# The expert step of a hybrid decoder layer, its order on five engines, and where the routing lists are written

## The reference

```python
def swiglu(x, wg, wu, wd):
    return (jax.nn.silu(x @ wg) * (x @ wu)) @ wd
...
    eidx, ew = route(h2d, w_router, router_bias)
    ffn = routed_experts(h2d, eidx, ew, w_exp_gate, w_exp_up, w_exp_down) + swiglu(h2d, w_sh_gate, w_sh_up, w_sh_down)
    return layer_norm(DEEPNORM_ALPHA * h + ffn.reshape(B, L, D), ln2_g, ln2_b)
```

## Time and profile before

| | us |
|---|---|
| median of 3 runs (lowest, highest) | 1830.36 (1829.62, 1830.92) |
| the profiled execution, its time | 1829.32 |
| its span in the trace | 1827.7 |
| trunk's last product ends, experts' first starts | 1015.7, 1016.9 |
| last gate-up product ends | 1714.1 |

### The profile page before, as it was taken

How to read it: one execution, slowest core, us unless ns; L and a number is a source line. 1 busy time by engine, 2 the same in 40 slices (tenths; PEclk the granted TensorE clock), 3 DMA queues, 4 the chain that set the end, 5 groups by cost and what they waited for, 6 DMA issues and landing times. The chain is left out here.

```text
span 1827.7 us, 26841 instructions
## 1 busy us (share of the span) xinstructions
PE 1750.7 (96%) x9506; PEld 1346.2 (74%) x9506; DVE 1078.4 (59%) x1711; ACT 692.7 (38%) x1110; POOL 322.8 (18%) x286
## 2 busy tenths in 40 slices
PE   7999999999999999999999968999999999999897
PEld 7999999999855556998876546676767767676532
DVE  3112442544346555655678537777777777777478
ACT  3112222222245455111111326565656656565222
POOL 0000320412100000001055512111121221121101
PEclk9999999999999999999999989999999999999998
DMA  6332543434213123634251789999999999999395
GB/s 212 96 94 79 167 121 113 147 104 134 89 50 93 46 59 143 233 108 149 70 214 28 271 282 352 392 383 402 403 392 389 387 397 388 396 388 372 142 421 236
DMA packets 131599, 408.55 MB, mean 224 GB/s; under 512 B 21748, under 2 KB 83348, under 8 KB 112916
## 3 DMA queue, kind: packets, MB, share of 16 engines
q1 hardware_dynamic: 107172, 337.93, 50.7%
q0 software_dynamic: 21472, 52.59, 7.5%
q10 hardware_dynamic: 2880, 17.04, 2.3%
HBM read 359.70 MB, written 67.80 MB: 234 GB/s over the span
## 5 line engine op out<-in xcount | busy, mean ns | idle before, releaser
L2501 PE MATMUL e_Y<-mixT,e_aT 128*128 128x512 f32 x544 | 252.0, 607 | 22.2 <-ACT e_aT L2343 22.2
L2510 PE MATMUL e_G<-w_lo,xT_hi 128*128 128x512 f32 x528 | 206.5, 391 | 0.0
L2501 PEld LDWEIGHTS e_Y<-mixT,e_aT 128*128 128x128 f32 x544 | 100.7, 195 | 125.2 <-issue 124.9
L2424 DVE TENSOR_TENSOR w_lo<-wb,e_w_hi 128x1024 fp32r<-128x1024 f32 x132 | 152.9, 1220 | 31.0 <-ACT e_w_hi L2352 31.0
L2424 DVE TENSOR_TENSOR w_lo<-wb,half_hi 128x1024 fp32r<-128x1024 f32 x128 | 148.3, 1220 | 32.5 <-ACT half_hi L2352 32.5
L1292 PE MATMUL banks<-x_hi,gw_hi 128*128 128x352 f32 x464 | 151.6, 327 | 1.4 <-DVE r_srg L1084 1.4
L181 PE MATMUL banks<-w_hi,x_hi 128*128 128x244 f32 x512 | 143.0, 279 | 9.9 <-DVE x_lo L235 8.8
L1292 PE MATMUL banks<-x_hi,gw_lo 128*128 128x352 f32 x464 | 148.8, 321 | 0.0
L1292 PE MATMUL banks<-x_lo,gw_hi 128*128 128x352 f32 x464 | 148.8, 321 | 0.0
L181 PE MATMUL banks<-w_hi,x_lo 128*128 128x244 f32 x512 | 142.1, 278 | 0.0
L181 PE MATMUL banks<-w_lo,x_hi 128*128 128x244 f32 x512 | 141.8, 277 | 0.0
(11 more groups left out here) (426 smaller groups left out, 3633.3 us busy)
## 6 DMA issues: line engine op xcount, KB each, us to landing
wb<-in_w_exp_gu SPq DMA_DIRECT2D x64, 2048.0 KB, 16.2
mixT<-in_w_exp_dn SPq DMA_DIRECT2D x68, 1024.0 KB, 10.8
yk<-d_y_rows SPq DMA_DIRECT2D x8, 3072.0 KB, 22.4
gw_sb<-in_w_gate SPq DMA_DIRECT2D x20, 512.0 KB, 6.6
d_proj<-o_sb SPq DMA_DIRECT2D x8, 1098.0 KB, 6.0
d_gateT<-r_g_out ACTq DMA_DIRECT2D x16, 528.0 KB, 2.6
pages<-in_cache_both SPq DMA_DIRECT2D x64, 128.0 KB, 2.0
wb<-in_w_exp_gu ACTq DMA_DIRECT2D x4, 2048.0 KB, 15.9
```

Of the source, the lines that this page charges most:

```text
L2424: v.tensor_tensor(w_lo[s][:, :, at_k, :], w_gu[s][:, :, at_k, :], w_hi[c][:, :, at_k, :].bitcast(F32), ALU.subtract).then_inc(w_lo_ok, 1)
L2501: mm = t_.matmul(Y[q][:], aT[:, c, k, :], w_d[:, s, k, q * 512:(q + 1) * 512], start=k == 0, stop=k == 1)
L2510: mm = t_.matmul(G[c], x[:, c, k, :], w[:, :, k, :], start=k == 0 and i == 0, stop=k == KD - 1 and i == 2)
```

## The change

Five things are altered.

1. PE's order: a pass is now G(e) with A(e-1) inside it, before the seventh of the eight K slices (`TURN_AT = 6`); then Y(e-1); then T(e+2). ACT and DVE follow: ACT rounds xT of e+1, copies Y(e-2), makes two casts of the weights of e+1, copies `aT`, makes the other two casts, then the sigmoid of e. DVE makes the rest of xT, copies its half of Y(e-2), makes `w_lo` and then the gate's products.
2. Scatters: 42 instead of 36 stand in trunk ahead of the gathers, and the last 12 after them, still in trunk. None is left in `experts`.
3. Trunk gathers four experts instead of three. In `experts` each gather is one further ahead.
4. Trunk's SP also loads the first four down weights and the two vectors of the last layer norm, which stood at the start of `experts`.
5. The overflow lists: SP loads all 52 that there could be, one after each refill of experts 8 to 59, each with a reading of `meta`. DVE waits for them before the pass of experts 60 to 63, not before that of 16 to 19. POOL waits for no list.

```diff
+            sp.dma_start(g1, a["ln2_g"].partition_broadcast(P)).then_inc(ln2_in, 16)
+            sp.dma_start(b1, a["ln2_b"].partition_broadcast(P)).then_inc(ln2_in, 16)
...
+            sp.wait_ge(up_done, 3)
+            sp.wait_ge(r_done, NT)
+            for s in range(4):
+                sp.dma_start(w_d[:, s].rearrange("p k n -> p (k n)"), a["w_exp_dn"][s]).then_inc(d_in[s], 16)
...
+            def listing(t):
+                for k in range(TOPK):
+                    g.indirect_dma_start(tok_list, bass.IndirectOffsetOnAxis(ap=slot_c[:, t, k:k + 1], axis=0), entry[:, t, k, :], None).then_inc(listed, 16)
...
+            for t in range(NT - 2):
                 if t % G == 0:
                     pool.wait_ge(slot_ok, t // G + 1)
-                for k in range(TOPK):
-                    g.indirect_dma_start(tok_list, bass.IndirectOffsetOnAxis(ap=slot_c[:, t, k:k + 1], axis=0), entry[:, t, k, :], None).then_inc(listed, 16)
+                listing(t)
             for s in range(3):
                 pool.wait_ge(h_out_s[s], 48)
             pool.wait_ge(l_done, NT // G)
-            for s in range(3):
+            for s in range(4):
                 pool.wait_ge(g_ok, s + 1)
                 g.indirect_dma_start(xg[s][:], None, h_rows, bass.IndirectOffsetOnAxis(ap=g_idx[s][:, 0:1], axis=0), bounds_check=XT - 1, oob_is_err=False).then_inc(x_in_e[s], 16)
+            listing(NT - 2)
+            listing(NT - 1)
...
-                for s in range(3):
+                for s in range(4):
                     v.tensor_copy(g_idx[s][:], list_g[:, s:s + 1]).then_inc(g_ok, 1)
...
-            for s in range(W):
-                down(s, s)
-            sp.dma_start(early[:, 0:D], a["ln2_g"].partition_broadcast(P)).then_inc(ln2_in, 16)
-            sp.dma_start(early[:, D:2 * D], a["ln2_b"].partition_broadcast(P)).then_inc(ln2_in, 16)
             more = quads(sp)
...
-                free = sp.snap(r * W + (s - W + 1))
+                free = at(sp, r, W, s - W + 1)
                 wait_alone(sp, gu_done, free)
                 gate_up(e, s)
                 wait_alone(sp, d_done, free)
                 down(e, s)
-            with sp.Fori(1, NE // W) as r:
+            def overflow_list(b):
+                first = number(sp, b, 1, LIST - P)
+                sp.dma_start(over[:, bass.ds(b, 1), :].rearrange("p o two -> p (o two)"), tok_list[bass.ds(first, P), :]).then_inc(over_in, 16)
+            for s in range(W):
+                refill(1, s, W + s)
+            sp.wait_ge(listed, 16 * TOPK * NT)
+            sp.wait_ge(over_clear, 1)
+            with sp.Fori(2, OVER // W + 2) as r:
                 for s in range(W):
                     refill(r, s, sp.snap(r * W + s))
+                    overflow_list(sp.snap(r * W + (s - 2 * W)))
+            for s in range(W):
+                refill(NE // W - 1, s, NE - W + s)
             with sp.Fori(NE // W, more + NE // W) as r:
                 for s in range(W):
                     refill(r, s, number(sp, sp.snap(r * W + (s - NE)), 0, NE - 1))
...
             for s in range(W):
-                gather(s + 4, (s + 3) % W, 2 * s if s else None)
+                gather(s + 5, s, 2 * s + 2)
                 if s >= 2:
                     put_rows(s - 1, s % 2, s - 2)
-                if s < 3:
-                    t = NT - 3 + s
-                    for k in range(TOPK):
-                        g.indirect_dma_start(tok_list, bass.IndirectOffsetOnAxis(ap=slot_c[:, t, k:k + 1], axis=0), entry[:, t, k, :], None).then_inc(listed, 16)
-            pool.wait_ge(listed, 16 * TOPK * NT)
-            pool.wait_ge(over_clear, 1)
-            with pool.Fori(0, more) as r:
-                for s in range(W):
-                    first = number(pool, pool.snap(r * W + s), 1, LIST - P)
-                    pool.dma_start(over[:, bass.ds(pool.snap(r * W + s), 1), :].rearrange("p o two -> p (o two)"),
-                                   tok_list[bass.ds(first, P), :]).then_inc(over_in, 16)
-                wait_alone(pool, over_in, pool.snap(r * (16 * W) + 16 * W))
...
-                    gather(at(pool, r, W, s + 4), (s + 3) % W, at(pool, r, 2 * W, 2 * s))
+                    gather(at(pool, r, W, s + 5), s, at(pool, r, 2 * W, 2 * s + 2))
                     put_rows(at(pool, r, W, s - 1), s % 2, (s - 2) % W)
...
-            gather(at(pool, r, W, 4), 3, at(pool, r, 2 * W, 0))
...
-            def rounded(s, n_in, c):
+            def rounded(s, n_in, c, part):
                 act.wait_ge(gu_in[s], n_in)
-                for j in range(4):
+                for j in (2 * part, 2 * part + 1):
                     s_.copy(w_hi[c][:, :, 2 * j:2 * j + 2, :], w_gu[s][:, :, 2 * j:2 * j + 2, :]).then_inc(w_hi_ok, 1)
...
             def four(r, last=False):
                 for s in range(W):
-                    c = s % 2
-                    turned_act(at(act, r, W, s - 1), c)
...
-                    turned(at(act, r, 2 * W, 2 * s + 2), c)
+                    c, n_in = s % 2, at(act, r, 16, 16 if s < W - 1 else 32)
+                    if not (last and s == W - 1):
+                        turned(at(act, r, 2 * W, 2 * s + 4), 1 - c)
                     kept(at(act, r, W, s - 1), c, at(act, r, 8 * W, 16 * (s // 2) - 16))
                     if not (last and s == W - 1):
-                        rounded((s + 1) % W, at(act, r, 16, 16 if s < W - 1 else 32), 1 - c)
+                        rounded((s + 1) % W, n_in, 1 - c, 0)
+                    turned_act(at(act, r, W, s), 1 - c)
+                    if not (last and s == W - 1):
+                        rounded((s + 1) % W, n_in, 1 - c, 1)
+                    gate(at(act, r, W, s + 1), c)
...
-                    if s == 0:
-                        take(at(dve, r, W, 3), 3, at(dve, r, 16, 0))
-                    else:
-                        take(at(dve, r, W, s + 3), s - 1, at(dve, r, 16, 16))
-                    gated(at(dve, r, W, s), 1 - c)
-                    turned(at(dve, r, W, s + 1), c)
+                    if not last:
+                        take(at(dve, r, W, s + 4), s, at(dve, r, 16, 16))
+                    if not (last and s == W - 1):
+                        turned(at(dve, r, W, s + 2), 1 - c)
...
                         residue(at(dve, r, W, s), (s + 1) % W, 1 - c)
-            with dve.Fori(1, 4) as r:
+                    gated(at(dve, r, W, s + 1), c)
...
-            dve.wait_ge(over_ok, 1)
+            dve.wait_ge(over_in, 16 * OVER)
...
-            with dve.Fori(4, more + (NE // W - 1)) as r:
+            with dve.Fori(NE // W - 1, more + (NE // W - 1)) as r:
...
-            def gate_up(n, c, s, n_in):
...
                 for k in range(KD):
+                    if k == TURN_AT:
+                        turn_act(at(pe, n, 1, -1), 1 - c, at(pe, n, 1, -2))
                     for i, (x, w) in enumerate(((xT_hi, w_hi[c]), (xT_hi, w_lo[s]), (xT_lo, w_hi[c]))):
                         mm = t_.matmul(G[c], x[:, c, k, :], w[:, :, k, :], start=k == 0 and i == 0, stop=k == KD - 1 and i == 2)
                 mm.then_inc(gu_done, 1)
...
+            pe.wait_ge(xT_act, 2)
+            turn(2, 16, None)
             pe.wait_ge(gu_in[1], 16)
-            pe.wait_ge(xT_act, 2)
             for k in range(KD):
+                if k == TURN_AT:
+                    turn_act(1, 0, 0)
                 mm = t_.matmul(G[1], xT[:, 1, k, :], w_gu[1][:, :, k, :], start=k == 0, stop=k == KD - 1)
             mm.then_inc(gu_done, 1)
-            turn_act(1, 0, 0)
+            down(1, 0, 0, 16, 0)
+            turn(3, 16, 1)
...
-                    c, now, last = s % 2, at(pe, r, 16, 16), at(pe, r, 16, 0)
-                    turn(s, c, now, at(pe, r, W, s - 2))
-                    down(at(pe, r, W, s - 1), c, (s - 2) % W, last if s < 2 else now, at(pe, r, W, s - 2))
-                    gate_up(at(pe, r, W, s + 1), c, s, now)
-                    turn_act(at(pe, r, W, s), 1 - c, at(pe, r, W, s - 1))
+                    c = s % 2
+                    gate_up(at(pe, r, W, s + 1), c, s)
+                    down(at(pe, r, W, s), 1 - c, (s - 1) % W, at(pe, r, 16, 16 if s else 0), at(pe, r, W, s - 1))
+                    if not (last and s >= 2):
+                        turn((s + 2) % W, at(pe, r, 16, 16 if s < 2 else 32), at(pe, r, W, s))
+            with pe.Fori(1, more + (NE // W - 1)) as r:
+                four(r)
+            four(pe.snap(more + (NE // W - 1)), last=True)
```

78 lines of the change are left out of this document (34 added, 44 removed).

## The result

The changed kernel takes **1817.65 us** (median of 5 runs, 1814.44 to 1822.42) where the kernel before takes 1830.36 (1826.36 to 1832.97): a ratio of **0.9936, 95% interval 0.9908 to 0.9963**. That is 12.7 us less, where I had forecast 20.8 less. The time is inside the range of 1802 to 1821, in its upper half.

What follows compares the result with a forecast made beforehand. PE bounds mid-stage, with DMA close to its end; the first steps lose 28.9 us through waits on POOL's lists. The terms -28.9 + 4.1 + 2.5 + 0.5 + 1.0 = -20.8 give 1809.5 us, range 1802 to 1821.

Steps and rivals of the forecast that it cites:

- Part 1: Experts' first six steps: with the lists out of POOL's way there, the 28.9 us lost go; -28.9 us.
- next in line: Experts' first steps: down weights, expert 4's gate-up weights and PE's first result rows, the next that could be late.
- Part 2: Trunk's end: POOL's twelve scatters behind the gathers make PE start experts later; +4.1 us, bounds 2.5 and 6.6.
- The clock: Start of experts: after PE's idle time its clock runs at the lower level; +2.5 us, bounds 0 and 3.1.
- Part 3: Order of a step in experts: two more transpose/product borders, 0.01 us in each of 66 steps; +0.5, up to 2.0.
- Part 4: Weight stream in experts: list loads on SP make it late by up to 5 us near the end; +1.0, bounds 0 and 5.
- the case: Whole kernel: the forecast's own sum, 1809.5 us, from 1804 to 1818 with all bounds together; chance 0.64.
- B: Rival, start of experts: the late start doesn't happen and the clock holds; 1803 to 1806 us, chance 0.10.
- A: Rival, later half of experts: the weight stream falls 11 us short, casts wait for `wb`; 1816 to 1826 us, chance 0.12.
- D: Rival, SP's queue: list loads hold up the weights and the kernel gets slower, about 1857 or 1841 us; chance 0.04.
- C: Rival, experts' first steps: a new wait for rows queued behind scatters and down weights; 1815 to 1823 us, chance 0.08.
- E: Rival, experts' first steps: the three waits for rows stay, coming from DMA contention; 1834 us or so, chance 0.02.

Runs made afterwards that it cites:

- first comparison: The changed kernel against the kernel before, ahead of the twelve follow-up kernels, on a chip without a recorded number; 1817.65 against 1830.36 us, ratio 0.9936.
- e4: The changed kernel's order of the step, with lists, scatters and down weights where the kernel before had them; ratio to the kernel before 0.9994.
- e6: The kernel before's order of the step and of the row gathers, with everything else as in the changed kernel; ratio to the kernel before 0.9990.
- e8: The changed kernel with 6 of the last 12 scatters in the experts' first three steps, two behind each gather; 1823.37 us, ratio to the kernel before 0.9926.
- e1: The changed kernel with its last 12 scatters in the experts' first three steps, four behind each gather; 1827.99 us, ratio to the kernel before 0.9937.
- e5: The changed kernel once more, with nothing but a comment added; 1837.14 us, ratio to the kernel before 0.9990.
- e9: The kernel before once more, with a comment added, in the last group; ratio to the same kernel 0.9983.
- e12: The changed kernel once more, in the last group; ratio to the kernel before 0.9969.
- e7: The changed kernel with the last 12 scatters four behind each of the experts' first three gathers and only the 4 needed lists loaded; ratio to the kernel before 0.9945.
- e11: The changed kernel with the last 12 scatters three behind each of the experts' first four gathers, only 4 lists loaded; 1824.73 us, ratio to the kernel before 0.9906.
- e2: The changed kernel with the four down weight loads (4 MB) back at the start of the experts; 1831.64 us, ratio to the kernel before 0.9959.
- the three groups: Twelve follow-up kernels in groups of four on chips 7, 14 and 4, each beside the kernel before, which took 1839.4, 1839.4 and 1839.9 us.

## Why the prediction was right, and where it was wrong

**Part 1, the first steps: right, -28.9.** In the first comparison all of it went. The lists did it and not the order (e4 and e6, each with one of the two). Of what I had named as next in line nothing came late: rows, down weights and gate-up weights were there in time.

**Part 2, the late start: the step that failed.** I had +4.1 with bounds of 2.5 and 6.6, and it is +11.1 (1027.97 - 1016.90). POOL's issuing was foreseen to end at 1018.2 plus 0 to 4, and it ended at 1019.4 (the last scatter starts at 1018.46 and takes 0.96). What I left out is that the trunk's exit is not open when POOL has issued its last indirect DMA, but 6.0 to 10.7 us after the start of that issue; in the sum "POOL ends at 1018.2" stood for the end of the drain. e8 and e1 show it by dose: with 12, 6 and 0 scatters behind the gathers PE idles for 9.4 (e5), 1.2 and 1.6 us at the exit. The record of before alone would have given it: my own sum has the last scatter start at 1018.2 + 1.6 - 1.3 = 1018.5, and 1018.5 + 7.2 + 1.2 - 1016.9 = 10.0.

The clock: 2.5 forecast. T took 1.94 instead of 1.04, and the 12 records of G(1) until A 6.92 instead of 5.15 (e1 has 5.15 without the idle time): 2.6, as forecast. What I had not booked is the other end: behind the stage the lower level lasted 3.4 us instead of 6.8, and the end of the program is 1.8 shorter.

**Part 3, the order: right.** Forecast +0.5. It is 66 x 0.02 = +1.3 in the steps and -0.9 in the last two, +0.4.

**Part 4, the weights: inside its bounds, but not at the place I had.** Forecast +1.0 with bounds 0 and 5, and 2.7 was measured, 0 to 4.7 in the other kernels with the same list loads. I had SP's gap as 5.2 us each time, and the loss near the stage's end, from a growing backlog. The gap is 5.4 at the median but goes up to 10.7, and 1.6 of the 2.7 us are lost in the three steps from 1139 to 1171, behind the largest gaps. The rest lies in ten steps between 1391 and 1523, ahead of which no gap is over 7 us; what made those longer is open. Nothing is lost after them. By the Trainium skill, "DMA: Bandwidth & Descriptors", Latency and other measured facts, the floor of a register load is 0.6 us; the smallest of the 52 gaps, each with two of them, is 3.9 us, so none of the readings here came near that floor. The landing times rise as in the earlier trace rows: gate-up loads landed after 10.5 us near 1095 and 21.8 at the median near 1610, where no step is longer than usual.

So -28.9 + 11.1 + 2.6 + 0.4 + 2.7 - 1.8 = -13.9, where the span has -14.0. That the time still fell into the case's own 1804 to 1818, at its upper edge, is in part luck: the late start passed its bound by 4.5 us, the other terms stayed inside theirs, and the 1.8 that came back was in no sum.

**The rivals.** B is excluded by the start. A and D ask for a loss of 11 us or more in the weight stream; no run has over 4.7. C and E would show waits for rows in the first steps, and there is none. None of them happened: the time came out between the forecast and A through a term that no rival held, the drain.

**What stays open.** In the two later groups that repeat it (chips 14 and 4) the same change is worth 0.1 and 0.3%, with intervals from -0.03 to 0.5%, so the 0.6% of the first comparison should not be carried to other chips. Where the gain went can be read: of the span's 14.0 us only 3.6 are left (e9 to e12), 7.8 less between Y(0) and Y(67), mostly because the kernel before loses less in its first steps, 1.4 more at the start of Y(0) and 1.2 less behind the stage. Why ACT stands there is not settled. It happens in all runs of the groups with three or more scatters in a step (e1, e4, e7, e9, e11; 3.7 to 10.5 us idle) and in none with two or none; and in all seven with scatters behind the gathers PE waits 2.2 to 4.1 us ahead of G(0) where the other five have 1.15. So scatters have a part in it, and the stop moves with them. They are not enough: the kernel before has six a step in the first comparison too, and no such wait stands in either of its traces. Which resource they share with ACT no run shows.

## What to carry to other kernels

Work moved ahead of a barrier is paid until the queue's drain has ended, 6 us or more behind the last issue here, and not until it has been issued. Before moving a queue's work to the end of a block, read when the drain of that queue ended in the trace of before, and whose end hides it. An idle moment made so can cost twice: behind the 12.7 us here the clock was at its lower level, which cost another 2.6 us. Work that nobody needs soon is best spread thin, a few DMAs a step, rather than put on either side of a border: with six there and two a step PE idled 1.2 to 2.0 us at the exit and no early step was longer, while twelve on either side cost 4 to 14 us.

## What the runs showed of the hardware that was not expected

- GpSimd's DRAIN at the trunk's exit ended 7.0 to 7.8 us after the start of its last gather (six traces), 6.0 after its last scatter with no large load beside it (e2 alone), and 8.1 to 10.7 where 4 MB of weights were loaded beside the last scatters (seven traces).
- ScalarE stood idle ahead of its copy of `aT` with nobody named as releaser, in the three groups and not in the first comparison: 0, 3.7, 7.8 to 8.0, 9.6 to 10.5 us with two, three, four and six scatters in the step. Counted from the end of the transposes that it copies, that is 3.4 us at three, 6.9 and 7.1 at four, 8.7 and 5.4 at six, where e9 has a second stop of 8.5.
- The same change gained 0.6% in the first comparison and 0.1 and 0.3% in two of the later groups, on the chips numbered 14 and 4. The kernel before took 9 us more in all three groups, and in e9 Y(0) came 19.9 us later and six steps took 8.3 us less.
- 52 loads of 1 KB with two register reads each, in the queue of a stream at 395 GB/s, cost between 0 and 4.7 us in all. Reads and load together held SP for 3.9 to 10.7 us.
